# Combine before gather at the end of each expert in a two-layer mixture-of-experts step

## The chip, the cores and the metric

The kernel runs on one core of one Trainium2 chip. The metric is the device time of one execution in microseconds (us); lower is better. The median of three runs of the kernel before is 2045.48 us.

## The reference, cut to what matters

One step of a two-layer model over 288 tokens (256 of a prompt, 32 new ones of 8 sequences), all in float32. Each layer is attention and then a feed-forward part. In the second layer that part is a mixture of 8 experts, and only it is touched here: each token goes to its two best experts, and each expert adds its result, weighted by the token's gate.

```python
def moe_swiglu(h, w_router, b_router, w_in, w_out):
    logits = jnp.einsum('btd,de->bte', h, w_router, preferred_element_type=F32) + b_router.astype(F32)
    top_v, top_i = lax.top_k(logits, TOP_K)
    gates = jax.nn.softmax(top_v, axis=-1)
    dense_gate = jnp.sum(jax.nn.one_hot(top_i, N_EXPERTS, dtype=F32) * gates[..., None], axis=-2)
    out = jnp.zeros(h.shape, F32)
    for e in range(N_EXPERTS):
        out = out + dense_gate[..., e:e + 1] * swiglu(h, w_in[e], w_out[e]).astype(F32)
    return out.astype(h.dtype)
```

Sizes: D_MODEL 1024, F_EXPERT 3584, N_EXPERTS 8, TOP_K 2. The weights of one expert are 21 pieces of 2 MB.

## The kernel before, in words

The program of each engine is written out by hand, with semaphores between them. Layer 0, the attention of layer 1 and the router come first; the experts start some 930 us into the span and end near 2006 us.

**Weights.** SyncE (SP) streams the 21 pieces of each expert into 7 slots of 2 MB, 14 pieces of w_in (line 581) and then 7 of w_out (line 585). A piece is requested as soon as TensorE has used the piece that held its slot. It waits for nothing of the gather or the combine.

**One expert on TensorE** (`expert`, lines 1400 to 1423 of the kernel before):
- It waits until ScalarE and VectorE have copied the expert's gathered tokens out of PSUM (semaphores `e_gcpA`, `e_gcpV`), reads the number of its tokens into a register (`value_load`, line 1405: the instruction TENSOR_LOAD and some register work), and takes a branch to one of three bodies (lines 1420 and 1421). They stand one behind the other in the program: P for up to 128 tokens, CAP for up to 144, and a narrow one for up to 64. Every expert has its own copy of all three. So from a body to the next expert's body TensorE's instruction stream jumps over up to two bodies; only from a narrow body to a following P body does the program simply go on. At the end of a P or CAP body stands one jump more, to the end of the expert.
- The body: gate and up projections (`ffn_in`; matmuls of line 1315 in the wide bodies P and CAP, of line 1297 in the narrow one), the transposes of the choice (`turn_choice`), and the out projection (line 1365 wide, 1349 narrow).
- The end: the **gather** of the next expert's tokens, then for a wide body `out_transposes` (lines 1377 and 1379), then the **combine**.

**The gather** (lines 1257 to 1266) multiplies the stored tokens by a 0/1 choice matrix into PSUM banks 0 to 2: 24 matmuls. In float32 each one shows as two MATMUL rows and two LDWEIGHTS rows, so 48 of each. It needs only the choice (`e_pick`), which VectorE makes in the middle of the expert. `gather_copy` on ScalarE (line 1767, two copies) and on VectorE (line 2283, one) brings it to SBUF as `hsel` and counts up `e_gcpA` and `e_gcpV`.

**The combine** (lines 1382 to 1398) multiplies the expert's output by the turned choice, 8 matmuls (16 in CAP), and VectorE adds each of the 8 results to `fT` (line 2313). It starts when the output is in `otok`, scaled by the gates: ScalarE and VectorE first copy the out projection's PSUM (`oeT`: for a wide body the source of the transposes; a narrow body doesn't use it), then wait for `e_tp`, then write `otok` and count up `e_ocA` and `e_ocV`. In a wide body `e_tp` comes from the last transpose, in a narrow one from the gather's first matmul, since TensorE works in order. From the fourth combine matmul on each waits for an add, as three banks go round.

Experts 0 to 7 (e0 to e7) of this input take these bodies: P, narrow, narrow, CAP, narrow, P, narrow, narrow. The last expert also gathers once (for a ninth expert that holds no token); then the final norm follows.

Of the kernel before, what the change touches and what calls it, by code (L numbers as in the profile page):

```python
# [171 lines left out]
def build(nc, t_in, t_out):  # L172
# [12 lines left out]
    with ctx:  # L185
# [134 lines left out]
        def bank(i, n=512, at_=0, rows=P):  # L320
            return ps[0:rows, 512 * i + at_:512 * i + at_ + n]

        ident = cst[:, C_ID:C_ID + 128]
        ones = cst[:, C_ONE:C_ONE + 128]
# [39 lines left out]
        e_oeA, e_oeV, e_tp = sem("e_outT_copied_act"), sem("e_outT_copied_vec"), sem("e_out_tokens_ready")  # L364
# [316 lines left out]
        def _(pe):  # L681
            mm, tp = nc.tensor.matmul, nc.tensor.transpose
# [78 lines left out]
            for k in range(KD):  # L761
                if k >= 2:
                    pe.wait_ge(x_cp, k - 1)
                for t, (t0, n) in enumerate(TILES):
                    last = tp(bank(k % 2, n, t0), xtok[0:n, t, 128 * k:128 * k + 128], ident[0:n, 0:n])
                last.then_inc(x_tp, 1)
            pe.wait_ge(c_silu, 1)
            for k in range(KD):
                last = tp(bank(2, 9, 9 * k), cstok[:, 128 * k:128 * k + 128], ident[0:9, 0:9])
# [17 lines left out]
            for hp in range(4):  # L787
                b = t_bank()
                for q in range(4):
                    h, c = 2 * hp + q // 2, q % 2  # L790
                    last = tp(bank(b, 128, 128 * q, 64), kvb[:, c, 128 * h:128 * h + 64], ident)
# [11 lines left out]
            for j, w in enumerate((384, 288, 512, 512, 512)):  # L803
                landed("in_ab", j)
                wt = chunk("in_ab", j, 0, 8 * w).rearrange("p (k m) -> p k m", k=KD)
                for t, (t0, n) in enumerate(TILES):
                    if nz >= 4:
                        pe.wait_ge(z_cp, nz - 3)
                    for k in range(KD):
                        if nz == 0:  # L810
                            pe.wait_ge(h_done, k + 1)
                        if n < P:
                            last = sample_rows(nz % 4, hT[:, k, t0:t0 + n], wt[:, k, :], w, k, KD)
                        else:
                            last = mm(bank(nz % 4, w), hT[:, k, t0:t0 + n], wt[:, k, :], start=(k == 0), stop=(k == KD - 1))  # L815
# [22 lines left out]
            for t in range(2):  # L838
                for hh in range(2):
                    for k in range(3):  # L840
                        last = mm(bank(2 * t + hh, 384), qnT[:, k, 128 * t:128 * t + 128], wt[:, k, 384 * hh:384 * hh + 384],
                                  start=(k == 0), stop=(k == 2))
                    last.then_inc(q_done, 1)
            pe.wait_ge(q_cp, 1)
            for k in range(3):
                for g in range(4):
                    last = mm(piece(0, g, 192), qnT[:, k, NTP:NT], wt[:, k, 192 * g:192 * g + 192], start=(k == 0), stop=(k == 2))
# [315 lines left out]
            for h in range(HA):  # L1163
# [3 lines left out]
                for c in range(2):  # L1167
                    last = mm(ps[r:r + 64, 512 * (h % 4):512 * (h % 4) + NT], kvb[:, c, 128 * h + 64:128 * h + 128],
                              qlT[:, c, h, :], start=(c == 0), stop=(c == 1))
# [6 lines left out]
            for j in range(11):  # L1176
                landed("ffd_in", j)
                w = chunk("ffd_in", j, 0, 4096).rearrange("p (g k m) -> p g k m", g=2, k=KD)
                for fb in range(2):
# [3 lines left out]
                    for g in range(2):  # L1183
                        for k in range(KD):
                            if f == 0 and g == 0:
                                pe.wait_ge(h_done, 8 + k + 1)
                            last = mm(bank(2 * (f % 2) + g, NT), w[:, g, k, 128 * fb:128 * fb + 128], hT[:, k, :],  # L1187
                                      start=(k == 0), stop=(k == KD - 1))
# [7 lines left out]
            for j in range(3):  # L1196
                landed("qkv_c", j)
                wt = chunk("qkv_c", j, 0, 4096).rearrange("p (k m) -> p k m", k=KD)
                for t, (t0, n) in enumerate(TILES):
                    if nz >= 19:  # L1200
                        pe.wait_ge(z_cp, nz - 3)
                    for k in range(KD):
                        if nz == 15:
                            pe.wait_ge(h_done, 16 + k + 1)
                        if n < P:
                            last = sample_rows(nz % 4, hT[:, k, t0:t0 + n], wt[:, k, :], 512, k, KD)
                        else:
                            last = mm(bank(nz % 4), hT[:, k, t0:t0 + n], wt[:, k, :], start=(k == 0), stop=(k == KD - 1))  # L1208
# [25 lines left out]
            for t, (t0, n) in enumerate(TILES):  # L1234
                for k in range(KD):
                    if t == 0:
                        pe.wait_ge(h_done, 24 + k + 1)
                    last = mm(bank(0, 8, 8 * t, n), hT[:, k, t0:t0 + n], wrout[:, k, :], start=(k == 0), stop=(k == KD - 1))
            last.then_inc(lg_done, 1)
            for t, (t0, n) in enumerate(TILES):  # L1240
                for kk in range(2):
# [3 lines left out]
                    for k in range(4):  # L1245
                        last = tp(bank(4 + i % 2, 128, 128 * k, n), hT[:, 4 * kk + k, t0:t0 + n], ident)
                    last.then_inc(htok_tp, 1)
            pe.wait_ge(msk_done, 1)
            for t in range(3):
                for tt in range(t + 1):  # L1250
                    last = mm(bank(1, 8, 8 * t), cst[:, C_UP:C_UP + 128] if tt == t else ones, mask[:, tt, :],
                              start=(tt == 0), stop=(tt == t))
            for tt in range(3):
                last = mm(bank(1, 8, 24), ones, mask[:, tt, :], start=(tt == 0), stop=(tt == 2))
            last.then_inc(pos_done, 1)

            def gather(idx, tokens_ready=False):

                pe.wait_ge(e_pick, idx)
                for k in range(KD):  # L1260
                    for t, (t0, n) in enumerate(TILES):
                        last = mm(bank(G_BANK[k // 3], CAP, CAP * (k % 3)), htok[t][:, 128 * k:128 * k + 128],  # L1262
                                  pick[:, t, 0:CAP], start=(t == 0), stop=(t == 2))
                        if tokens_ready and k == 0 and t == 0:
                            last.then_inc(e_tp, 1)
                last.then_inc(e_gat, 1)

            def turn_choice(it, cols):
# [103 lines left out]
            def out_transposes(it, cols):  # L1372

                pe.wait_ge(e_oeA, it + 1)
                pe.wait_ge(e_oeV, it + 1)
                for k in range(KD):
                    last = tp(bank(5 + k // 4, 128, 128 * (k % 4)), oeT[:, k, 0:P], ident)
                for k in range(KD if cols > P else 0):
                    last = tp(bank(3 + k // 4, 128, 128 * (k % 4), EXTRA), oeT[:, k, P:CAP], ident)
                last.then_inc(e_tp, 1)  # L1380

            def combine(it, cols):

                pe.wait_ge(e_ocA, it + 1)
                pe.wait_ge(e_ocV, it + 1)
                for i, k in enumerate((0, 4, 1, 5, 2, 6, 3, 7)):
                    if i >= 3:
                        pe.wait_ge(e_add, NE * it + i)
                    out = bank((5, 6, 7)[i % 3], NT)
                    d = k // 4  # L1390
                    c0 = 128 * (k % 4)
                    if cols:
                        last = mm(out, otok[d][:, c0:c0 + 128], putT[0], start=True, stop=cols <= P)
                        if cols > P:
                            last = mm(out, rest_rows[:, 128 * k:128 * k + 128], rest_put, start=False, stop=True)
                    else:
                        last = mm(out, otok[0][64 * d:64 * d + 64, c0:c0 + 128], putT[0][64 * d:64 * d + 64, :], start=True, stop=True)
                    last.then_inc(e_cb, 1)

            def expert(it, e, p_):  # L1400

                pe.wait_ge(e_gcpA, it + p_ + 1)
                pe.wait_ge(e_gcpV, it + p_ + 1)
                own = cnt_i[0:1, bass.ds(e, 1)]
                tokens = pe.value_load(own, min_val=0, max_val=NT)

                def body(cols):

                    ffn_in(it, cols)
                    pe.wait_ge(e_pcp, it + 1)  # L1410
                    if cols:
                        wide_out(it, cols)
                    else:
                        narrow_out(it)
                    gather(it + p_ + 2, not cols)
                    if cols:
                        out_transposes(it, cols)
                    combine(it, cols)

                with pe.If(tokens > p_ * CAP + NARROW):  # L1420
                    with pe.If(tokens <= p_ * CAP + P):
                        body(P)
                    with pe.Else():
                        body(CAP)
                with pe.Else():
                    body(0)
# [396 lines left out]
        def _(dve):  # L1823
# [401 lines left out]
            for t, (t0, n) in enumerate(TILES):  # L2225
                last = V.max(top[0:n, t, :], logit[0:n, t, :])
# [56 lines left out]
            def gather_copy(idx):  # L2283
                dve.wait_ge(e_gat, idx)
                V.tensor_copy(hsel[:, 3:6, :], bank(G_BANK[1], 3 * CAP).rearrange("p (k n) -> p k n", k=3)).then_inc(e_gcpV, 1)

            def expert(it, e, p_, base):

                def turned_copy(j):
                    dve.wait_ge(e_t, FCH * it + (j + 1))  # L2290
                    V.tensor_copy(actT[:, j, :], bank(4, 256)).then_inc(e_tc, 1)

                for j in range(FCH):
                    if j:
                        turned_copy(j - 1)
                    if j == 4:
                        choose(e + 1, it + p_ + 1, it + 1, base)
                    for i, b in enumerate(E_BANK[j % 2]):
                        w = CAP if i else 256
                        dve.wait_ge(e_si, NFE * it + (4 * j + i + 1))  # L2300
                        out = act_b[:, j, i - 1, :] if i else act_a[:, j, :]
                        V.tensor_tensor(out, bank(b, w, 256), sil[i % 2][:, 0:w], ALU.mult).then_inc(e_act, 1)  # L2302
                turned_copy(FCH - 1)
                dve.wait_ge(e_o, FCH * it + (FCH + NMSLOT))
                V.tensor_copy(oeT[:, 3:6, :], bank(6, 3 * CAP).rearrange("p (k n) -> p k n", k=3)).then_inc(e_oeV, 1)  # L2305
                dve.wait_ge(e_pcp, it + 1)
                dve.wait_ge(e_tp, it + 1)
                V.tensor_scalar(otok[1], bank(6), gpl[:, 0:1], None, ALU.mult)
                V.tensor_scalar(otok[2][:, 512:1024], bank(4, 512, 0, EXTRA), gpl[0:EXTRA, 1:2], None, ALU.mult).then_inc(e_ocV, 1)
                gather_copy(it + p_ + 2)  # L2310
                for i, k in enumerate((0, 4, 1, 5, 2, 6, 3, 7)):
                    dve.wait_ge(e_cb, NE * it + (i + 1))
                    V.tensor_tensor(fT[:, k, :], bank((5, 6, 7)[i % 3], NT), fT[:, k, :], ALU.add).then_inc(e_add, 1)

            def pass_body(it0, p_, base):

# [63 lines left out]
```

## Time and profile before

| | us |
|---|---|
| runs: median, lowest, highest | 2045.48, 2031.88, 2050.39 |
| profiled execution: span from first to last instruction | 2039.5 |
| median of the runs less that span | 6.0 |
| TensorE matmul busy | 1827.6 (90%) |
| VectorE, ScalarE busy | 418.7 (21%), 334.0 (16%) |
| chain that ended last: TensorE, DMA | 73%, 12% |
| mean granted TensorE clock, share of full speed | 0.953 |

The time of a run holds the span and what lies around it. The profile gives the span of the profiled execution alone, so the distance to the median of the runs stands for the rest.

How to read it: a busy share is an average over stages with different limits. In a chain of waits each piece begins where what released it ended; "issue" in it is time in which TensorE waited for nothing that shows as an engine's work. PE is the matmul side of TensorE, PEld its weight loads, PEldq its instruction sequencer, which handles waits, register loads and branches. DVE is VectorE, ACT is ScalarE. A timeline merges equal instructions: start, length, count, and in brackets how long the engine had stood idle and what ended that.

### The profile page before, as it was taken

How to read it: one execution, taken by the hardware profiler on the slowest of the kernel's cores; microseconds unless marked ns; L12 is line 12 of the kernel's file. 1: busy time of each engine (PE TensorE's matmuls, PEld its weight loads, DVE VectorE, ACT ScalarE, POOL GpSimd, SP SyncE). 2: the span in 40 equal slices, each digit the busy share in tenths (PEclk: the TensorE clock that was granted, in tenths of full speed). 3: DMA queues.
4: the chain of work that ended last, by engine and by line, in shares of the span. 5: the costliest groups of instructions: out<-in, count | busy, mean ns of one | idle time of the engine just before them, and what ended most of it. 6: DMA issues, size and time to landing. Idle time of an engine off the chain costs nothing.

```text
span 2039.5 us, 30167 instructions
## 1 busy us (share of the span) xinstructions
PE 1827.6 (90%) x12873; PEld 1354.7 (66%) x12874; DVE 418.7 (21%) x1260; ACT 334.0 (16%) x1000; POOL 53.2 (3%) x99
## 2 busy tenths in 40 slices
PE   6799899899999997988998979789989899988874
PEld 3455566667777745768997636389976499954532
DVE  1114333340000034642101211101012111021213
ACT  2122334230000123621000101000001000011102
POOL 1002120000000000000000000000000000000000
PEclk9998999799999997888999999989999999989997
DMA  9943866454334562052785999986749998869991
GB/s 352 366 135 109 274 215 226 150 190 141 124 105 128 165 211 80 31 218 83 278 314 194 385 397 388 402 326 248 289 167 355 399 361 311 307 239 402 386 401 40
DMA packets 252023, 504.30 MB, mean 247 GB/s; under 512 B 6953, under 2 KB 65497, under 8 KB 251746
## 3 DMA queue, kind: packets, MB, share of 16 engines
q1 hardware_dynamic: 248066, 495.49, 67.4%
q0 software_dynamic: 3808, 6.61, 1.1%
q8 instruction: 119, 1.95, 0.4%
q14 instruction: 30, 0.25, 0.0%
HBM read 499.05 MB, written 3.02 MB: 246 GB/s over the span
## 4 chain that ended last, share of the span: by engine, by line
PE 73%; DMA 12%; SPq 6%; issue 3%; DVE 3%; ACT 1%; POOL 0%; DVEq 0%
PE ps L1315 15%; PE ps L1187 8%; PE ps L1297 8%; PE ps L1365 8%; PE ps L755 7%; DMA big<-in_w_moe_out 6%; SPq L585 4%; PE ps L815 3%; DMA big<-in_w_ada 3%; PE ps L1262 3%; PE ps L1208 2%; DMA big<-in_w_moe_in 2%; PE ps L704 2%; PE ps L917 1%; PE ps L1349 1%
## 5 line engine op out<-in xcount | busy, mean ns | idle before, releaser
L1315 PE MATMUL ps<-big 128*128 128x128 f32 (+1 forms) x2688 | 315.7, 281 | 9.1 <-issue 9.1
L1315 PEld LDWEIGHTS ps<-big 128*128 128x128 f32 x2688 | 314.6, 193 | 10.2 <-issue 10.2
L1297 PE MATMUL ps<-big 128*64 128x256 f32 x2240 | 262.3, 392 | 45.0 <-issue 35.1
L1297 PEld LDWEIGHTS ps<-big 128*64 128x64 f32 x2240 | 163.1, 141 | 133.6 <-issue 51.3
L1187 PE MATMUL ps<-work,big 128*128 128x288 f32 x704 | 171.2, 406 | 1.0 <-ACT work L1462 1.0
L1462 ACT ACTIVATE gqkv<-ps 128x144 f32<-128x144 f32 (+1 forms) x231 | 66.5, 315 | 619.2 <-PE ps L1315 300.9
L2302 DVE TENSOR_TENSOR z<-ps,gqkv 128x256 f32<-128x256 f32 x224 | 69.0, 334 | 460.7 <-ACT gqkv L1462 460.7
L1349 PE MATMUL ps<-big,z 128*64 128x512 f32 x560 | 127.7, 598 | 38.2 <-DMA big<-in_w_moe_out 35.2
L1187 PEld LDWEIGHTS ps<-work,big 128*128 128x128 f32 x704 | 133.6, 190 | 38.3 <-issue 1.5
L1365 PE MATMUL ps<-z,big 128*128 128x128 f32 (+1 forms) x1344 | 155.6, 279 | 2.3 <-issue 2.3
L1365 PEld LDWEIGHTS ps<-z,big 128*128 128x128 f32 x1344 | 155.1, 191 | 2.8 <-issue 2.8
L1462 ACT ACTIVATE z<-ps 128x288 f32<-128x288 f32 (+5 forms) x107 | 43.9, 426 | 576.0 <-PE ps L1349 159.9
L1349 PEld LDWEIGHTS ps<-big,z 128*64 128x64 f32 x560 | 37.8, 136 | 122.1 <-issue 63.9
L704 PE MATMUL ps<-big,csT 128*32 128x256 f32 x576 | 67.5, 388 | 21.6 <-DMA big<-in_w_ada 20.1
L755 PE MATMUL ps<-z,big 128*128 128x288 f32 x352 | 85.6, 406 | 1.0 <-DVE z L2181 1.0
L1462 ACT ACTIVATE big<-ps 128x384 f32<-128x384 f32 (+11 forms) x137 | 56.0, 432 | 167.0 <-PE ps L704 63.7
L755 PEld LDWEIGHTS ps<-z,big 128*128 128x128 f32 x352 | 66.8, 190 | 19.8 <-DVE z L2181 1.4
L1462 ACT ACTIVATE work<-ps 128x288 f32<-128x288 f32 (+4 forms) x104 | 38.3, 394 | 193.3 <-PE ps L755 137.3
L704 PEld LDWEIGHTS ps<-big,csT 128*32 128x32 f32 x576 | 35.0, 112 | 49.3 <-DMA big<-in_w_ada 14.1
L755 PE MATMUL ps<-o_or_q,big 128*128 128x288 f32 x256 | 65.2, 418 | 0.6 <-ACT o_or_q L1462 0.6
L2305 DVE COPY z<-ps 128x432 f32<-128x432 f32 x8 | 4.9, 608 | 290.7 <-PE ps L1365 148.1
L815 PE MATMUL ps<-big,work 128*128 128x512 f32 (+2 forms) x160 | 60.6, 537 | 3.3 <-ACT work L1462 3.3
(319 smaller groups left out, 1646.4 us busy)
## 6 DMA issues: line engine op xcount, KB each, us to landing
big<-in_w_moe_in SPq DMA_DIRECT2D x112, 2048.0 KB, 15.6
big<-in_w_moe_out SPq DMA_DIRECT2D x56, 2048.0 KB, 19.6
big<-in_w_ada SPq DMA_DIRECT2D x24, 2048.0 KB, 13.6
big<-in_w_ffd_in SPq DMA_DIRECT2D x22, 1024.0 KB, 7.7
big<-in_w_ffd_out SPq DMA_DIRECT2D x8, 1408.0 KB, 7.0
big<-in_cache_b_k SPq DMA_DIRECT2D x4, 2048.0 KB, 8.1
big<-in_cache_mla_ckv SPq DMA_DIRECT2D x64, 128.0 KB, 4.2
big<-in_cache_b_v SPq DMA_DIRECT2D x4, 2048.0 KB, 11.9
```

The lines of the kernel that those rows point to most:

```text
L585: sp.dma_start(wslot(q).rearrange("p (f m) -> p f m", f=4), src).then_inc(e_in[q], 16)
L704: last = mm(ps[CB * g:CB * g + CB, 512 * b:512 * b + WA], csT[:, k, :], w[:, k, WA * g:WA * g + WA], start=(k == 0), stop=(k == KD - 1))
L755: last = mm(bank(4 + k % 2, NT), w[:, f, 128 * m:128 * m + 128], rhs[:, f, :], start=(f == 0), stop=(f == nk - 1))
L815: last = mm(bank(nz % 4, w), hT[:, k, t0:t0 + n], wt[:, k, :], start=(k == 0), stop=(k == KD - 1))
L1187: last = mm(bank(2 * (f % 2) + g, NT), w[:, g, k, 128 * fb:128 * fb + 128], hT[:, k, :], start=(k == 0), stop=(k == KD - 1))
L1262: last = mm(bank(G_BANK[k // 3], CAP, CAP * (k % 3)), htok[t][:, 128 * k:128 * k + 128], pick[:, t, 0:CAP], start=(t == 0), stop=(t == 2))
L1297: last = mm(ps[64 * a:64 * a + 64, 512 * b + 256 * g:512 * b + 256 * g + 256], hsel[:, k, 0:NARROW], w[:, k, 256 * a:256 * a + 256], start ...
L1315: last = mm(bank(b, cols, 256 * g), w[g][:, k, 128 * i:128 * i + 128], hsel[:, k, 0:cols], start=(k == 0), stop=(k == KD - 1))
L1349: last = mm(ps[64 * d:64 * d + 64, 512 * 5:512 * 6], actT[:, q, 128 * m + 64 * half:128 * m + 64 * half + 64], w[:, i, 512 * d:512 * d + 5 ...
L1365: last = mm(bank(5 + k // 3, cols, CAP * (k % 3)), w[:, i, 128 * k:128 * k + 128], act, start=(q == 0 and i == 0 and k % 3 == 0), stop=(q ...
L1462: return nc.scalar.activation(out, in_, f, **kw)
L2302: V.tensor_tensor(out, bank(b, w, 256), sil[i % 2][:, 0:w], ALU.mult).then_inc(e_act, 1)
```

## The change

At the end of every body TensorE now works out_transposes (wide bodies), then the combine, then the gather, so that the gather's matmuls stand directly ahead of the branch to the next expert. As the gather's first matmul came behind the narrow out projection and gave `e_tp`, a narrow body now has one small matmul of 4 columns in its place. VectorE does its 8 adds before its copy of the gather; ScalarE's order is unchanged.

```diff
-            def gather(idx, tokens_ready=False):
+            def gather(idx):
 
                 pe.wait_ge(e_pick, idx)
                 for k in range(KD):
                     for t, (t0, n) in enumerate(TILES):
                         last = mm(bank(G_BANK[k // 3], CAP, CAP * (k % 3)), htok[t][:, 128 * k:128 * k + 128],
                                   pick[:, t, 0:CAP], start=(t == 0), stop=(t == 2))
-                        if tokens_ready and k == 0 and t == 0:
-                            last.then_inc(e_tp, 1)
                 last.then_inc(e_gat, 1)
...
                         wide_out(it, cols)
                     else:
                         narrow_out(it)
-                    gather(it + p_ + 2, not cols)
                     if cols:
                         out_transposes(it, cols)
+                    else:
+                        mm(bank(4, 4), ident, ones[:, 0:4], start=True, stop=True).then_inc(e_tp, 1)
                     combine(it, cols)
+                    gather(it + p_ + 2)
...
                 V.tensor_scalar(otok[2][:, 512:1024], bank(4, 512, 0, EXTRA), gpl[0:EXTRA, 1:2], None, ALU.mult).then_inc(e_ocV, 1)
-                gather_copy(it + p_ + 2)
                 for i, k in enumerate((0, 4, 1, 5, 2, 6, 3, 7)):
                     dve.wait_ge(e_cb, NE * it + (i + 1))
                     V.tensor_tensor(fT[:, k, :], bank((5, 6, 7)[i % 3], NT), fT[:, k, :], ALU.add).then_inc(e_add, 1)
+                gather_copy(it + p_ + 2)
```

TensorE at the end of a narrow body, here of e4, and at the start of e5, before the change. 64x512 are the last matmuls of the out projection, 128x144 those of the gather, 128x288 those of the combine; in brackets the semaphores that an instruction waits for.

```order
L1349 MATMUL ps<-big,z 64x512 x7
L1262 MATMUL ps<-o_or_q,work 128x144 [waits pick_ready]
L1262 MATMUL ps<-o_or_q,work 128x144
...
L1397 MATMUL ps<-big,work 128x288 [waits e_out_copied_vec,e_out_copied_act]
L1397 MATMUL ps<-big,work 128x288 x2
L1397 MATMUL ps<-big,work 128x288 [waits combine_added] x5
L1425 UNCONDITIONAL_BRANCH
L1405 TENSOR_LOAD work [waits gather_copied_vec,gather_copied_act]
```

The same place with the change.

```order
L1347 MATMUL ps<-big,z 64x512 x7
L1416 MATMUL ps<-cst 128x4
L1395 MATMUL ps<-big,work 128x288 [waits e_out_copied_vec,e_out_copied_act]
L1395 MATMUL ps<-big,work 128x288 x2
L1395 MATMUL ps<-big,work 128x288 [waits combine_added] x5
L1262 MATMUL ps<-o_or_q,work 128x144 [waits pick_ready]
L1262 MATMUL ps<-o_or_q,work 128x144
...
L1262 MATMUL ps<-o_or_q 128x144
L1425 UNCONDITIONAL_BRANCH
L1403 TENSOR_LOAD work [waits gather_copied_vec,gather_copied_act]
```

The gather (24 matmuls) has moved from ahead of the combine to behind it; the read of the count still waits for the gather's copies, and these now follow the last thing that TensorE does in the body.

VectorE at the end of the first expert, before and with the change as one piece of the difference: L2308 and L2309 write `otok`, L2285 copies the gather, the eight 128x288 are the adds.

```order
 L2308 TENSOR_SCALAR work<-ps,work 128x512
 L2309 TENSOR_SCALAR work<-ps,work 16x512
+L2312 TENSOR_TENSOR work<-ps,work 128x288 x8
 L2285 COPY big<-ps 128x432
-L2313 TENSOR_TENSOR work<-ps,work 128x288 x8
 L2302 TENSOR_TENSOR z<-ps,gqkv 128x256
```

The copy of the gather has moved behind the adds, as the gather has on TensorE.

## Rows read from the trace of the kernel before

**Rows 1.** Page, head: the span of the profiled execution.

```profile
span 2039.5 us, 30167 instructions
```

**Rows 2.** Timeline, TensorE, end of e0 (P) and start of e1 (narrow).

```profile
1101.35 1.04 PE L1377 MATMUL ps<-cst,z 128*128 128x128 f32 x8
1104.04 4.12 PE L1393 MATMUL ps<-big,work 128*128 128x288 f32 x16 [1.65 <-DVE work L2309]
1115.73 1.55 PE L1297 MATMUL ps<-big 128*64 128x256 f32 x6 [7.58 <-issue]
```

**Rows 3.** Chain that ended last, end of e1 (narrow): start us, us, what.

```profile
1202.49 6.08 PE ps L1262 x48
...
1209.80 2.41 PE ps L1397 x10
1212.21 6.37 issue
1218.58 4.60 PE ps L1297 x27
```

**Rows 4.** The same chain behind the combines of e2, e3, e4, e5.

```profile
1325.23 6.61 issue
...
1519.69 6.33 issue
...
1623.54 0.39 issue
...
1789.03 7.35 issue
```

**Rows 5.** By source line, TensorE's sequencer, e0, e1, e3: ns min/median/max, first and last start.

```profile
L1421 PEldq COMPARE_BRANCH  x1: 3639/3639/3639, 1107.2 to 1107.2; - x1
...
L1420 PEldq COMPARE_BRANCH  x1: 3941/3941/3941, 1111.7 to 1111.7; - x1
...
L1405 PEldq TENSOR_LOAD <-work x1: 311/311/311, 1211.6 to 1211.6; - x1
...
L1420 PEldq COMPARE_BRANCH  x1: 6287/6287/6287, 1212.2 to 1212.2; - x1
...
L1423 PEldq COMPARE_BRANCH  x1: 3641/3641/3641, 1517.3 to 1517.3; - x1
```

**Rows 6.** Windows: DMA and granted clock at e0/e1, over e2, behind the router's gather.

```profile
core 0: us, PE busy (x) PEld busy (x) DVE busy (x) ACT busy (x) POOL busy (x), PEclk, DMA share, GB/s
1104.20:1120.00 15.80, 8.22 (x42) 5.31 (x43) 3.87 (x9) 0.23 (x1) 0.00 (x0) 0.78 0.02 4
...
1198.80:1311.90 113.10, 91.06 (x649) 51.84 (x649) 17.85 (x52) 10.94 (x38) 0.00 (x0) 0.97 1.04 394
...
941.50:944.90 3.40, 3.40 (x16) 3.40 (x17) 0.00 (x0) 0.00 (x0) 0.00 (x0) 0.50 0.00 0
...
1204.10:1208.00 3.90, 3.90 (x34) 3.90 (x33) 0.35 (x1) 0.39 (x1) 0.00 (x0) 1.00 1.05 387
```

**Rows 7.** Timeline, ScalarE at the end of e1: the `oeT` copies, then `otok`.

```profile
1202.54 0.83 ACT L1462 ACTIVATE z<-ps 128x432 f32<-128x432 f32 x2 [30.60 <-PE ps L1349]
...
1203.26 1.23 ACT L1462 ACTIVATE work<-ps,work 128x512 f32<-128x512 f32 x2
```

**Rows 8.** Timeline behind the router's gather, ahead of e0: its copies, e0's first matmuls.

```profile
939.32 0.83 ACT L1462 ACTIVATE big<-ps 128x432 f32<-128x432 f32 x2 [11.25 <-PE ps L1262]
...
941.42 0.92 PE L1315 MATMUL ps<-big 128*128 128x128 f32 x3 [2.14 <-issue]
```

**Rows 9.** A wait on TensorE's sequencer in e0, and the chain there.

```profile
L1279 PEldq EVENT_SEMAPHORE  x1: 2865/2865/2865, 1042.4 to 1042.4; - x1
...
1044.60 0.77 issue
```

**Rows 10.** Timeline, e2: the first matmuls that wait for weights.

```profile
1265.15 3.67 PE L1297 MATMUL ps<-big 128*64 128x256 f32 x32 [1.38 <-DMA big<-in_w_moe_in]
```

**Rows 11.** Timeline behind the last combine: ScalarE's squares, VectorE's first step of the final norm.

```profile
2006.95 2.77 ACT L1462 ACTIVATE work<-work 128x288 f32<-128x288 f32 x8 [3.30 <-DVE work L2313]
2008.13 0.35 DVE L1879 TENSOR_SCALAR work<-work,coef 128x256 f32<-128x256 f32 x1 [1.22 <-ACT work L1462]
```

## The prediction

> **What bounds the kernel now.** I read the head of the page for the span [rows 1], then the chain of waits through the experts, then the ends of single experts in the timeline, and last the rows of TensorE's own sequencer. In the chain the reader is to see that behind nearly every combine TensorE stands idle for 6.3 to 7.6 us under the name "issue" [rows 2 to 4]; behind e4 alone it is 0.39 us [rows 4], and e4, a narrow body, is the one that a P body follows, so that nothing is jumped over. The sequencer's rows say what "issue" is: a taken branch. The one at the end of e0 took 3.64 us and the one into e1's narrow body 3.94 us, both while the weight stream stood still (a DMA share of 0.02); the one from e1 into e2 took 6.29 us, with the stream at full load (1.04) [rows 5, 6]. The change removes none of these jumps; what counts is when each can begin.
>
> Two facts decide that. First, the sequencer runs ahead of the matmuls where nothing holds it: it stood at a wait at 1042.4 while the matmuls ahead of that wait ended at 1044.60, 2.2 us later [rows 9], and at the end of e3 it took its branch at 1517.3 while the combine ended at 1519.69, 2.4 us later [rows 4, 5]. I use 2.3 us. In e0's combine the waits for the adds hold it longer: its branch came at 1107.2, 0.95 us ahead of the combine's end at 1108.15 (7.58 ahead of 1115.73) [rows 2, 5]. Second, it can't read the next count before the gather's copies are done. Before the change these are long done when the combine ends.
>
> The weights matter too. From the end of e1 to that of e2 the DMA share is 1.04 throughout [rows 6], and e2 waits for its weights from 1265.15 on [rows 10]: a later start of e2 is caught up in these waits. e6 and e7 stand to each other in the same way (two narrow bodies in a row). All other ends have a wide body on one side or the final norm behind, and there a delay goes into the time.
>
> **The change part by part.** Nothing is removed but the order; 5 matmuls of 4 columns are added, which I cost at nothing, since ScalarE's `oeT` copies cover them (0.83 us [rows 7]).
>
> *What the gather hid.* Before, its 6 us lay over the copies of the out projection. Now they stand open.
> - Narrow: the out projection of e1 ends at 1202.49; `otok` is written from 1203.26 for 1.23 us, so until 1204.49, and 0.15 us later the combine can start: 2.1 us in which TensorE waits [rows 3, 7].
> - Wide: one pair of `oeT` copies, 0.83 us (the same copies as in rows 7), and some 0.3 us of latencies and lost overlap: 1.1 us. The wait behind the transposes, 1.65 us, stood open before [rows 2].
>
> So the combine and the gather together end 2.1 us (narrow) or 1.1 us (wide) later than before.
>
> *What now stands ahead of the branch.* With the gather last, the read of the count comes 0.9 us behind the gather's end: two copies of ScalarE, 0.83 us, with latencies [rows 8].
> - Narrow, with a jump: before, the read began at 1211.6, 0.6 us ahead of the end at 1212.21 [rows 3, 5]. Now it begins 0.9 us behind an end that is itself 2.1 us later: 0.6 + 0.9 + 2.1 = 3.6 us. The jump is as long as before, as the stream is at full load there before and after.
> - Narrow with no jump (e4): the same 3.6, and the 2.14 us of idle that the router's gather shows between gather and body [rows 8] hold 0.2 us more than the read took in e4: 3.8.
> - P: the jump at the end now stands behind matmuls that wait for nothing but the choice, so the sequencer comes to it 2.3 us ahead of the gather's end instead of 0.95 ahead of the combine's. Its start moves by 1.1 - 2.3 + 0.95 = -0.25 us. It takes 3.64, so it ends 1.3 us behind the gather, when the copies (0.9) are done: they cost nothing here. Everything behind it is as before: -0.3 each.
> - CAP: there the sequencer was 2.4 us ahead already: 1.1 - 2.3 + 2.4 = +1.2.
> - Behind e7: ScalarE now copies the gather before its squares. The combine ended near 2006.1, so the gather ends near 2008.2 and the copies at 2009.1, against squares from 2006.95 [rows 11]. VectorE's start moves by about as much: +2.1.
>
> The nearest row for the run-ahead is the one of e3, at the same kind of place; the bounds are that none of it comes (the jump starts with the gather's end, and a P end costs +2.0 instead of -0.3) and that all of it is hidden (the read starts 0.9 behind the gather, -0.7).
>
> The Trainium skill, "Advanced Engine Details and Errata", section "Engine Queue Depths", gives TensorE a queue of 64 instructions. The gather is 96 rows in 5.9 us, so 64 of them would let the sequencer be about 3.9 us ahead, an estimate from that page; the rows show 2.2 to 2.4. By the page the three wide ends would each be 0.6 us shorter and the sum 1.8 us smaller; I stay with the rows.
>
> *The clock.* After the long gaps it is at 0.5 before and after alike. But the new waits are new idle time in a stretch that ran at 1.00 [rows 6]. After the 2.14 us of idle behind the router's gather the clock stood at 0.50 for 3.4 us [rows 6, 8], which costs 1.7 us of work; after the 1.65 us in e0 it did not fall before the next long gap, and over e2, with its many waits for weights (the first 1.38 us [rows 10]), its mean is 0.97. My new idles are 2.1 us at e2, e4 and e7, 2.1 us ahead of e5's body, and at e0 and e5 1.0 and 1.65 us close together. So 0 to 6 times 1.7 us, and as they lie nearest to the row of 2.14 but not surely alike, I take three: 5.1 us.
>
> *Sum.* e0 and e5 -0.6, e2 +3.6, e3 +1.2, e4 +3.8, e7 +2.1, clock +5.1: about +15 us. e1 and e6 (+3.6 each) cost nothing as long as the weights cover them. On the span of 2039.5 that makes 2054.5; the median of the runs lies 6.0 above this span, so 2060.5. Without the clock it would be +10, with all six falls +20.
>
> **The rivals.**
> 1. *The sequencer doesn't get ahead of the gather* (or the jump into the next body gets longer). For it: the gather is short pieces with a weight load each, and no row shows the sequencer passing just these. Against it: rows 5 and 9. The three wide ends then cost 2.3 us more each, and up to 3.6 if the fetch also waits on the copies: +7 to +11, so about 2070.
> 2. *The weights don't cover e1 and e6.* For it: e2 has slack only until 1265. Against it: it comes to the weights' pace 46 us behind its start at 1218.58 and goes at that pace for 46 us more, up to 1311.9. +7.2: about 2068.
> 3. *Not slower: the branch is taken during the gather.* Were the count read and the jump begun while the gather still runs, its 6 us would cover the fetch at every end. A narrow end with a jump would then take 2.1 + 3.6 + 6 + 0.9, some 12.7 us instead of 16.1 (1202.49 to 1218.58 [rows 3]): -3.4 at e2. At a wide end 1.1 + 0.9 stand in place of the idle behind the combine [rows 4]: -5.6 and -5.4 at e0 and e5, -4.3 at e3. With e4 (2.1 + 0.9 for 0.39, +2.6) and e7 (+2.1) still dearer the sum is -14 us: 2031.5. It decides where the read of the count doesn't wait for the copies. For it: the first jump of a wide end does come early. Against it: the order shows the read waiting for both copies, and behind the router's gather the body began only 2.14 us later with no jump at all [rows 8].
>
> **How the numbers follow.** My forecast, +15 with +8 to +21 as its own range, gets 0.70; the first rival 0.12, the second 0.08, the third 0.06; 0.04 is left for what I don't see. The range reaches from 2046 (little loss of clock, quick fetches) to 2076 (the first rival with most falls of the clock); the runs of before alone are 18 us apart. Over 1%, some 20 us, is about what a measurement of this kernel can tell from no change. The forecast lies under it, so its upper end (0.08) and the two slow rivals make slower 0.28; the third rival's -14 is within 1%, and faster gets 0.03; the same 0.69.
>
> **What would show it.** In the profile of the changed kernel: the combine of a narrow body starts 2.1 us behind the out projection; the count is read 0.9 us behind the gather's end, never before; the branch at the end of e0 begins some 2.3 us ahead of that end and takes 3.6; idle between gather and next body is about 8 us behind e1 and e2 (0.9, 0.7 for the read, 6.3), 6 us behind e0, 2.1 us behind e4; e2 and e7 end no later against their predecessors than before. I am wrong if the branch into a body starts before the gather's copies are done, if the fetches change their length, or if e2's end moves with its start.

## The result, and the profile after

The changed kernel takes 2057.55 us (median of 4 runs, 2053.88 to 2066.97) against 2040.8 us before (4 runs, 2031.88 to 2050.39): the medians are 16.75 us apart, a quotient of 1.0082, and the ratio on record is 1.0101 with a 95% interval of 1.0055 to 1.0148. Measured again beside other kernels on one chip (6 runs against 17, below) the ratio is 1.0102, 1.0078 to 1.0125, with medians of 2061.51 and 2036.93, 24.6 us apart. The ratio on record is not the quotient of the medians, and the record does not say how it is formed; by either the kernel is about 1% slower. The span of the profiled execution went from 2039.5 [rows 1] to 2054.3 us, by 14.8. The time of that same execution is 2055.88, only 1.6 us above its span; the 6.0 us that the forecast put between span and time were for the most part the spread of the runs.

The end of e1 in the chain of waits of the changed kernel, to be held against [rows 3] (start us, us, what):

```profile
1196.21 3.68 PE ps L1347 x16
...
1200.34 0.40 ACT z L1462
1200.74 1.13 ACT work L1462 x2
1201.87 0.10 issue
1201.97 0.78 PE ps L1395 x4
...
1203.24 2.41 PE ps L1395 x10
1205.65 6.09 PE ps L1262 x48
...
1212.19 0.41 ACT big L1462
1212.61 7.04 issue
1219.65 2.40 PE ps L1295 x9
```

ScalarE's copies now stand in the chain, first those of the out projection (2.1 us from 1199.89 to the combine at 1201.97), then those of the gather; before, the gather lay over the ones and the combine over the others. From the end of the out projection to the next body's first matmul it is 19.8 us, where it was 16.1. The sequencer's rows behind it, and the jump at the end of e0, answer to [rows 5] (ns min/median/max, first and last start):

```profile
L1421 PEldq COMPARE_BRANCH  x1: 3472/3472/3472, 1104.6 to 1104.6; - x1
...
L1403 PEldq TENSOR_LOAD <-work x1: 308/308/308, 1212.6 to 1212.6; - x1
...
L1420 PEldq COMPARE_BRANCH  x1: 6205/6205/6205, 1213.4 to 1213.4; - x1
```

The count is read at 1212.6, 0.9 us behind the gather's end (1205.65 + 6.09 = 1211.74), and the jump behind it is as long as it was (6.2). At the end of e0 the jump starts at 1104.6, while the gather runs on to 1106.98; it is done 1.1 us behind it. The end of e0 in the timeline, against [rows 2]:

```profile
1096.97 4.12 PE L1391 MATMUL ps<-big,work 128*128 128x288 f32 x16 [1.65 <-DVE work L2309]
...
1113.18 1.12 PE L1295 MATMUL ps<-big 128*64 128x256 f32 x4 [6.21 <-issue]
```

The idle ahead of e1 is 6.21 instead of 7.58 us; most of the difference stands ahead of the combine now, where the copies of the out projection are open: behind the out projection combine and gather together take 13.67 us (1093.31 to 1106.98) instead of 12.52 (1095.63 to 1108.15), 1.15 more.

This table has, for every expert, the time from the end of its out projection to the next body's first matmul (for e7: to the end of the span), worked out from the timelines of the two profiles in the same way (the changes from hundredths).

| end | body, next body | before | after | change | forecast |
|---|---|---|---|---|---|
| e0 | P, narrow | 20.1 | 19.9 | -0.2 | -0.3 |
| e1 | narrow, narrow | 16.1 | 19.8 | +3.7 | +3.6, covered |
| e2 | narrow, CAP | 16.3 | 20.0 | +3.6 | +3.6 |
| e3 | CAP, narrow | 23.6 | 24.2 | +0.6 | +1.2 |
| e4 | narrow, P | 10.1 | 16.3 | +6.2 | +3.8 and clock |
| e5 | P, narrow | 19.9 | 22.8 | +2.9 | -0.3 and clock |
| e6 | narrow, narrow | 16.1 | 19.8 | +3.7 | +3.6, covered |
| e7 | narrow, final norm | 42.8 | 45.0 | +2.2 | +2.1 |

The cover held: from the end of e1's out projection to that of e2's it is 113.0 us in both profiles, and the weight stream runs at a share of 1.04 over that stretch in both [rows 6]. In what follows a fall is a stretch in which the granted clock is at 0.50, the lower of its two levels (1.2 and 2.4 GHz). The clock's part is seen in windows of the changed kernel (busy us and count of PE, PEld, DVE, ACT, POOL, then granted clock, DMA share, GB/s), to be held against [rows 6]:

```profile
1618.30:1625.00 6.70, 6.70 (x23) 5.06 (x22) 3.31 (x8) 0.00 (x0) 0.00 (x0) 0.50 1.05 387
...
1631.90:1635.20 3.30, 3.30 (x17) 3.30 (x17) 0.00 (x0) 0.00 (x0) 0.00 (x0) 0.50 1.05 387
1788.90:1795.60 6.70, 6.05 (x13) 4.36 (x14) 2.79 (x6) 0.34 (x1) 0.00 (x0) 0.50 0.64 244
```

The clock is at 0.50 in e4's combine and the start of its gather, at the start of e5's body and in e5's combine. In the chain these two ends read:

```profile
1617.47 4.84 PE ps L1395 x16
1622.31 7.45 PE ps L1262 x48
...
1789.55 7.16 PE ps L1391 x16
1796.71 5.89 PE ps L1262 x48
```

In e1 the same pieces took 3.68 and 6.09 us, and in e0 the combine 4.12: 2.5 us lost at e4 and 3.0 at e5. e5's body took 154.2 us instead of 152.6, 1.6 more. So of the 14.8 us, 7.1 are these three falls, and -0.2 + 3.6 + 0.6 + 3.7 (e4 without its fall) - 0.1 (e5 without its fall) + 2.2 = 9.8 are the order; the rest, -2, lies where the change isn't: e0's body had a fall of 1.6 in the profile before [rows 6] and none in the one after, and the experts began 0.7 us earlier.

### The profile page after: what moved, and what is told of

Its sections match the earlier page's. It is cut to its first block, busy times and chain, and to the rows that moved or that the text cites. A ratio compares the mean times of both kernels' runs of the same rounds, so it can differ in the third digit from the quotient of the medians.

```text
span 2054.3 us, 30187 instructions
## 1 busy us (share of the span) xinstructions
PE 1833.2 (89%) x12883; PEld 1362.7 (66%) x12884; DVE 419.5 (20%) x1260; ACT 334.4 (16%) x1000; POOL 53.3 (3%) x99
## 3 DMA queue, kind: packets, MB, share of 16 engines
q0 software_dynamic: 3808, 6.61, 1.1%
## 4 chain that ended last, share of the span: by engine, by line
PE 71%; DMA 12%; SPq 8%; issue 4%; DVE 3%; ACT 2%; POOL 0%; DVEq 0%; ACTq 0%
PE ps L1313 15%; PE ps L1187 8%; PE ps L1363 8%; PE ps L1295 7%; PE ps L755 7%; DMA big<-in_w_moe_out 6%; SPq L585 5%; DMA big<-in_w_ada 3%; PE ps L815 3%; PE ps L1262 3%; PE ps L1208 2%; DMA big<-in_w_moe_in 2%; PE ps L704 1%; PE ps L1347 1%; PE ps L1395 1%
## 5 line engine op out<-in xcount | busy, mean ns | idle before, releaser
L1313 PEld LDWEIGHTS ps<-big 128*128 128x128 f32 x2688 | 314.6, 193 | 12.7 <-issue 12.7
L755 PEld LDWEIGHTS ps<-z,big 128*128 128x128 f32 x352 | 66.8, 190 | 19.8 <-DVE z L2181 1.4
L704 PEld LDWEIGHTS ps<-big,csT 128*32 128x32 f32 x576 | 34.7, 112 | 50.6 <-DMA big<-in_w_ada 14.8
```

Source lines behind the costliest of these rows:

```text
L704: last = mm(ps[CB * g:CB * g + CB, 512 * b:512 * b + WA], csT[:, k, :], w[:, k, WA * g:WA * g + WA], start=(k == 0), stop=(k == KD - 1))
L755: last = mm(bank(4 + k % 2, NT), w[:, f, 128 * m:128 * m + 128], rhs[:, f, :], start=(f == 0), stop=(f == nk - 1))
L1313: last = mm(bank(b, cols, 256 * g), w[g][:, k, 128 * i:128 * i + 128], hsel[:, k, 0:cols], start=(k == 0), stop=(k == KD - 1))
```

## The experiments

**x1: the read of the count no longer waits for the gather's copies.**

```diff
-                pe.wait_ge(e_gcpA, it + p_ + 1)
-                pe.wait_ge(e_gcpV, it + p_ + 1)
                 own = cnt_i[0:1, bass.ds(e, 1)]
...
                 def body(cols):
 
+                    pe.wait_ge(e_gcpA, it + p_ + 1)
+                    pe.wait_ge(e_gcpV, it + p_ + 1)
                     ffn_in(it, cols)
```

> The changed kernel, with the wait for the gather's copies moved from ahead of the read of the count to the start of the next body. My theory: in the changed kernel the read is held by these copies, 0.9 us behind the gather's end. Without that wait it begins some 2.3 us ahead of the gather's end, as far as the sequencer gets ahead of the matmuls. A narrow end with a jump (e1, e2, e6: 19.7 to 20.0 us from the end of the out projection to the next body's first matmul) gets 3.2 us shorter, about 16.6; e4's end, with no jump, 1 to 1.3 us shorter without its clock loss; P and CAP ends stay within 0.3 us, since there the jump at the end of the body is what the read waits for. The time falls by some 4 to 5 us against the changed kernel, before the clock. Rival (the branch hides the whole fetch under the gather as soon as nothing holds the read): narrow ends 12.7 us, P ends 14.5 us. Rival (the read waits for the matmuls whatever the semaphores say): nothing changes.

One run: 2049.58 us, the kernel before beside it 2040.23. The end of e6 in the chain, and its read:

```profile
1895.88 6.09 PE ps L1262 x48
...
1902.84 3.87 issue
1906.70 3.65 PE ps L1295 x15
```

```profile
L1401 PEldq TENSOR_LOAD <-work x1: 306/306/306, 1899.6 to 1899.6; - x1
```

The read comes at 1899.6, 2.4 us ahead of the gather's end at 1901.97, and the end takes 16.6 us instead of 19.8, as my theory had it. The sequencer gets no further ahead than that, so the rival's 12.7 us is out, and so is the one that reads only behind the matmuls. The other ends are harder to tell: e0, e1, e2, e4 and e5 each had a fall here, and e1 and e2 took 19.4 us with theirs. The idle behind the gather shows the read's part all the same: at e0 and e5 it is 6.42 and 5.91 us, where the changed kernel has 6.21 and 6.10, so that the free read gives nothing there; ahead of e5's body it is 0.92 instead of 1.93. e3's end took 24.8, 0.6 more than in the changed kernel's first profile and outside what I expected; x8, which has no such edit, has 24.8 there too.

**x2: the same in the kernel before.** The edit of x1, made to the kernel before.

> The kernel before, with the same wait moved behind the branch. My theory: there the read is held not by the copies but by the combine's last wait for an add, so nothing moves: 20.1, 16.1, 16.3, 23.6, 10.1, 19.9, 16.1 us at the ends of e0 to e6, each within 0.3. Rival (the copies hold it in the kernel before too): the narrow ends get 1 to 2 us shorter.

One run: 2031.85 us beside 2040.23, within what single runs differ by. The ends of e0 to e6 took 19.9, 16.1, 16.3, 23.7, 10.1, 20.1 and 16.1 us: nothing moved. With the combine last it is not the copies of the gather that hold the sequencer. What is left are the combine's waits for the adds; that they do is argued from the order of the program, and no run took them out.

**x3: VectorE's half of the change alone.** `gather_copy` of VectorE behind its adds, TensorE as before.

```diff
-                gather_copy(it + p_ + 2)
                 for i, k in enumerate((0, 4, 1, 5, 2, 6, 3, 7)):
                     dve.wait_ge(e_cb, NE * it + (i + 1))
                     V.tensor_tensor(fT[:, k, :], bank((5, 6, 7)[i % 3], NT), fT[:, k, :], ALU.add).then_inc(e_add, 1)
+                gather_copy(it + p_ + 2)
```

> The kernel before, with VectorE's copy of the gather moved behind its 8 adds and TensorE's order as it was: the VectorE half of the change alone. My theory: the copy now ends some 0.45 + 0.6 us behind the combine, so the read of the count begins 1.1 us behind the combine's end and not 0.6 ahead of it: +1.7 us at the narrow ends (e1, e2, e4, e6: 17.8, 18.0, 11.8, 17.8 us); nothing at P and CAP ends, where the jump at the end of the body takes longer. On the time +3 to +4 us (e2 and e4; e1 and e6 are covered by the weights). Rival (the read isn't held by that semaphore): nothing moves.

One run: 2049.32 us beside 2040.23; the experts began 6 us later in this profile than in that of before, which the edit can't reach. The end of e1 in the chain:

```profile
1216.07 2.06 PE ps L1397 x8
1218.13 0.02 issue
1218.15 0.82 DVE work L2312 x2
1218.97 0.52 DVE big L2285
1219.50 7.13 issue
```

VectorE's copy now stands in the chain, behind the adds. The narrow ends took 17.9, 18.1, 11.9 and 17.8 us, the P and CAP ends 20.7, 23.6 and 19.7: +1.8 where the read is next, little where a jump stands ahead of it (e0's 0.6 us lies in jumps that took 3.79 and 4.39 instead of 3.64 and 3.94). From e0's first matmul to the end of the span this profile takes 1100.0 us, that of before 1098.1, of which 1.6 are its fall at e0: 3.5 more, where I expected 3 to 4. So the price of a held read is shown by itself.

**x4 and x9: the new idle times filled.** The changed kernel with matmuls whose results are not used, so that TensorE isn't idle there.

```diff
+            def fill(b, n):
+                for _ in range(n):
+                    mm(bank(b, 128), ident, ones, start=True, stop=True)
...
                     if cols:
+                        fill(0, 3)
                         out_transposes(it, cols)
+                        fill(0, 6)
                     else:
                         mm(bank(4, 4), ident, ones[:, 0:4], start=True, stop=True).then_inc(e_tp, 1)
+                        fill(0, 8)
                     combine(it, cols)
                     gather(it + p_ + 2)
+                    if not cols:
+                        fill(3, 8)
```

> The changed kernel, with small matmuls of no use put into its new idle times: 8 of 128 columns behind a narrow out projection and 8 behind a narrow body's gather, 3 and 6 around a wide body's transposes. They fill about 1.9, 1.9, 0.7 and 1.5 us and none is on the path. My theory: the clock falls at e4's combine, ahead of e5's body and at e5's combine come from the new idles; filled, the clock stays at 1.00 there, e4's end takes 13.6 to 13.9 us instead of 16.3, e5's body 152.6 instead of 154.2, e5's end 19.8 instead of 22.8: the span falls by about 7 us against the changed kernel, to some 2047. Rival (the falls have nothing to do with these idles): falls remain at such places, and the span stays near 2054.

One run: 2048.75 us beside 2040.23, span 2047.1. e4's end took 13.9 us, e5's body 152.6, e5's end 19.5. The clock stood at 1.00 over e4's end, at e5's start and over e5's end:

```profile
1615.70:1630.00 14.30, 14.04 (x102) 12.32 (x103) 5.71 (x12) 2.78 (x6) 0.00 (x0) 1.00 1.05 386
1630.00:1633.40 3.40, 3.40 (x33) 3.40 (x32) 0.00 (x0) 0.00 (x0) 0.00 (x0) 1.00 1.05 387
1782.20:1796.00 13.80, 13.04 (x90) 11.64 (x88) 5.79 (x12) 2.21 (x5) 0.00 (x0) 1.00 0.43 155
1329.80:1338.80 9.00, 6.68 (x26) 6.33 (x27) 0.00 (x0) 0.00 (x0) 0.00 (x0) 0.50 1.05 387
```

The last row is one I had not expected. Behind e2 the 8 matmuls keep TensorE at work 2 us longer into the gap, and the clock, which in the changed kernel is at 0.50 for the first 5.5 us of e3's body, is so for the first 9.1 here. But in the row the matmuls are busy for 6.68 of its 9 us only. The timeline shows why:

```profile
1329.79 3.46 PE L1317 MATMUL ps<-big 128*128 128x144 f32 x13 [6.32 <-issue]
1335.57 14.63 PE L1317 MATMUL ps<-big 128*128 128x144 f32 x104 [2.32 <-issue]
```

Behind the body's first 13 matmuls TensorE stands idle for 2.32 us under the name "issue"; in the changed kernel the first 142 run without a gap. The body took 173.7 us instead of 170.5. Of these 3.2 us the stop is 2.3; the low clock, under which TensorE works for 6.8 us instead of 5.5, costs half of the difference, 0.7. What makes the stop was not tried.

That the span fell to the 2047.1 that I expected is luck in part: the experts began 4.6 us earlier than in the changed kernel's profile (936.13 against 940.72). From e0's first matmul to the end of the span the two take 1111.0 and 1113.6 us. The three places gave back 7.4 us, as expected; e3's body took 3.2 of it, and a fall at the start of e0's body, which this profile has and the other not, 1.6.

Both kernels were then timed on one chip.

> The changed kernel once more, on the chip of the next run, for its time beside that of the filled kernel. My theory: the open copies and the later read cost 9.6 us in every execution, and the clock some 0 to 10 us more, as the new idle times meet it: a ratio of 1.007 to 1.009 over the kernel before. In its profile the segments stay (19.8 us at narrow ends with a jump, 19.9 at P ends without a fall), and the places of the falls may be others than in the first profile. Rival (the falls are tied to the places): the same three places again.

> The filled kernel of x4, now timed. My theory: without the clock's part it stands some 9 to 10 us over the kernel before, a ratio of 1.0045 to 1.005, and 3 to 7 us under the changed kernel beside it; no fall in its profile behind an out projection, at a combine or between e4's gather and e5's body. Rival (the useless matmuls cost as much as the clock they keep): the same time as the changed kernel.

| kernel | median (lowest to highest), runs | ratio to before | 95% interval |
|---|---|---|---|
| changed (x8) | 2061.51 (2055.65 to 2062.55), 6 | 1.0102 | 1.0078 to 1.0125 |
| changed, filled (x9) | 2049.27 (2040.28 to 2057.76), 12 | 1.0061 | 1.0039 to 1.0083 |
| before | 2036.93 (2027.32 to 2046.22), 17 | | |

Of the 1.0% the filling takes 0.4 back, some 8 us (12 between the medians). In the profiles, from e0's first matmul to the end, x8 takes 1117.5 us, x9 1109.1 and the kernel before 1098.1. I had expected a ratio of 1.0045 to 1.005 and 3 to 7 us less than the changed kernel, so both came out larger. What is left, 0.6% or 12 us, is the 9.8 of the order and the 3 us at e3: x9's profile has 173.5 us there, with a stop of 2.31 us behind the first 13 matmuls. In x8's profile, without filling, the falls stood at the same three places as in the first profile and at two more:

```profile
1621.00:1627.70 6.70, 6.70 (x23) 5.02 (x22) 3.37 (x8) 0.00 (x0) 0.00 (x0) 0.50 1.05 385
1634.70:1638.00 3.30, 3.30 (x17) 3.30 (x17) 0.00 (x0) 0.00 (x0) 0.00 (x0) 0.50 1.05 387
1791.70:1798.40 6.70, 6.12 (x13) 4.43 (x14) 2.72 (x6) 0.27 (x1) 0.00 (x0) 0.50 0.63 241
1904.30:1911.00 6.70, 6.66 (x23) 5.38 (x24) 2.82 (x7) 0.00 (x0) 0.00 (x0) 0.50 1.05 388
2016.90:2023.70 6.80, 6.77 (x24) 5.30 (x24) 3.00 (x8) 0.00 (x0) 0.00 (x0) 0.50 0.00 0
```

The two more are e6's end (covered by the weights) and e7's (not covered). x1, with the same idles ahead of its combines, had falls at e0, e1 and e2 too. So my ratio of 1.007 to 1.009 was a little low, and whether the three places come back in every execution stays open: two profiles of the changed kernel had them, and there are no more.

**x5: the gather in two parts.** 15 of its 24 matmuls stand ahead of the combine as before, 9 behind it. In a narrow body the first of them gives `e_tp` again.

```diff
...
+                    gather(it + p_ + 2, 0, 5, not cols)
                     if cols:
                         out_transposes(it, cols)
-                    else:
-                        mm(bank(4, 4), ident, ones[:, 0:4], start=True, stop=True).then_inc(e_tp, 1)
                     combine(it, cols)
-                    gather(it + p_ + 2)
+                    gather(it + p_ + 2, 5, KD)
```

> The gather in two parts: its first 15 matmuls (k 0 to 4) where the kernel before has the gather, the last 9 (2.2 us) behind the combine; the rest as in the changed kernel, with the read of the count behind the gather's copies. My theory: the first part hides the copies of the out projection, so combine and gather together end where they ended before (12.5 us behind the out projection at a P end, 9.7 at a narrow one); the read still comes 0.9 us behind the gather's end. So from the out projection's end to the next body: narrow 17.6 (16.1 before, 19.8 with the change), e4 11.9 (10.1, and 13.9 with the change without its clock loss), P 18.7 (20.1 and 19.8), CAP 23.6 (23.6 and 24.2). No clock falls at e4 or at the combines. Span about 1 us over the kernel before. Rival (what is dear is the order, combine ahead of any of the gather, not the open copies): the narrow ends stay near 19.8.

One run: 2039.78 us, beside 17 runs of the kernel before with a median of 2034.91. Ends of e0 to e6: 19.2, 17.9, 18.0, 23.6, 11.9, 18.4, 17.8 us. The 15 matmuls hide the copies, the combine starts at once, and the rival's 19.8 is out: it was the open copies. e0's end is 0.5 above the 18.7 that I expected. One miss: I expected no fall of the clock at e4, and one came at the start of e5's body, behind the 1.95 us of idle between this gather's end and that body (1621.80 to 1623.75 in the chain); e5's body took 154.2 us.

```profile
1619.38 2.42 PE ps L1263 x18
...
1622.66 1.09 issue
1623.75 2.42 PE ps L1317 x16
```

```profile
1625.30:1628.60 3.30, 3.30 (x18) 3.30 (x17) 0.00 (x0) 0.00 (x0) 0.00 (x0) 0.50 1.05 387
```

**x6: x5 with the read set free as in x1.**

> x5 with the wait for the gather's copies moved behind the branch. My theory: nothing then holds the sequencer in the last 2.2 us of a body: the read begins 2.3 us ahead of the gather's end. Narrow ends 14.5 us (16.1 before), P 18.6, CAP 23.6, e4 10.7 (its first matmul now waits for the copies themselves). Against the kernel before e0 and e5 -1.5 each, e2 -1.6, e3 0, e4 +0.6, e7 +0.4: about -3.5 us. Rival (a jump taken while matmuls run takes longer by as much): the narrow ends stay near 16.

One run: 2032.01 us, beside the same 17. Ends: 18.8, 14.6, 14.8, 23.8, 10.8, 18.5, 14.5 us. The end of e2 in the chain, and its read:

```profile
1316.08 2.42 PE ps L1263 x18
...
1319.36 3.97 issue
1323.33 2.74 PE ps L1317 x10
```

```profile
L1405 PEldq TENSOR_LOAD <-work x1: 304/304/304, 1316.0 to 1316.0; - x1
```

The read comes 2.5 us ahead of the gather's end at 1318.49, and the jump runs while matmuls do: 4.8 us of idle where the kernel before has 6.61 [rows 4]. Against the kernel before the ends of e0, e2 to e5 sum to -1.3 - 1.5 + 0.2 + 0.7 - 1.4 = -3.3 us. That is too little for its single time to tell.

**x7: x6 with all counts read ahead of e0.**

```diff
-                own = cnt_i[0:1, bass.ds(e, 1)]
-                tokens = pe.value_load(own, min_val=0, max_val=NT)
+                tokens = counts[e] if isinstance(e, int) else pe.value_load(cnt_i[0:1, bass.ds(e, 1)], min_val=0, max_val=NT)
...
+            counts = [pe.value_load(cnt_i[0:1, e:e + 1], min_val=0, max_val=NT) for e in range(3)]
             gather(1)
+            counts += [pe.value_load(cnt_i[0:1, e:e + 1], min_val=0, max_val=NT) for e in range(3, NE)]
```

> x6 with the counts of all 8 experts read once, ahead of the first expert, so that no read stands ahead of a branch. My theory: every end with a jump gets the read's 0.65 to 0.75 us shorter than in x6: narrow 13.8, P 17.9, CAP 22.9, e4 10.7. Against the kernel before about -6.5 us, a ratio near 0.997; the timing can hardly tell that from no change, the profile can. Rival (the jump's fetch begins only when the matmuls ahead of it have ended): no gain over x5.

2034.51 us (12 runs) against 2034.91 (17): a ratio of 0.9992, 0.9972 to 1.0013, no change that can be told, and no version of this study that beats the kernel before measurably. The narrow ends are 13.9 and 14.1 us as expected, but P and CAP ends gained nothing (19.1, 23.8, 18.7). Their second jump, now directly behind the first, takes longer:

```profile
L1422 PEldq COMPARE_BRANCH  x1: 4937/4937/4937, 1110.4 to 1110.4; - x1
...
L1423 PEldq COMPARE_BRANCH  x1: 3747/3747/3747, 1106.6 to 1106.6; - x1
```

4.94 us, against 4.31 in x6 and 3.94 in [rows 5], both with a read in between. What holds the second jump was not tried. And the early reads are not free: TensorE is idle for 4.89 us ahead of the router's gather, where it was 3.90 before and in x6, and from that gather's start to e0's first matmul it is 10.06 us instead of x6's 9.15. So x7 pays some 1.9 us ahead of e0, which I had not counted.

## Why the prediction was right, point by point

- **The forecast.** +15 us, 2060.5; measured +16.75 between the medians, 2057.55, ratio 1.0101, and +14.8 between the spans. The sign and most of the size, 9.8 of the 14.8 us, came from the order as it was said (10.1). That the whole fits so well is luck in part: the clock cost 2.0 us more than its term, and some 2 us were gained where the change is not.
- **The open copies and the held read** (+3.6 at a narrow end): +3.6 and +3.7 in the profile. x5 removes the one, x1 the other, x3 adds the read's wait to the kernel before; each moved the narrow ends by about what its part was said to cost (1.9, 3.2 and 1.8 us).
- **The sequencer 2.3 us ahead.** At the ends of e0, e3 and e5 the jump starts 2.35 us ahead of the gather's end, at e0 at 1104.6 against 1106.98. The rows were right to follow. The 3.9 us that were worked out, as an estimate, from the queue of 64 that the Trainium skill gives ("Advanced Engine Details and Errata", section "Engine Queue Depths") did not show in any run. The sum that the prediction hung on it is wrong besides: by its own terms the read would then wait for the copies, 0.9 us behind the gather instead of 1.34, so a wide end would be 0.45 us shorter, not 0.6, and the sum 1.3 us smaller. The first rival, no lead at all, is out: P ends moved by -0.2.
- **The cover of the weights.** The end of e2's out projection did not move against that of e1's, nor e7's against e6's (113.0 and 112.8 us, 113.0 and 112.9 before). The second rival is out.
- **The branch taken during the gather,** the third rival: out by the read at 1212.6; and x1 shows that even a free read would have given 3 us at a narrow end and nothing behind the gather of a P end; the lead of 2.4 us was as far as the sequencer got.
- **CAP** (+1.2): +0.6 in the first profile, where its two jumps took 3.28 and 3.86 instead of 3.64 and 4.16; +1.2 in x8's, with jumps of 3.57 and 4.25. The order's term fits; the length of a jump varies by some tenths, and two profiles can't tell more.
- **The clock** (+5.1, three falls of 1.7): this is the term that was mis-sized. Three falls it was, but those at e4 and in e5's combine lasted 6.8 us and cost 2.5 and 3.0; with the 1.6 at e5's start 7.1 us in the first profile, and 9.3 in x8's, with the 2.2 of e7's; there e6's body took 1.7 more besides, most of it as it began with 7.4 us at 0.50 instead of 4.1. That the idles cause them is shown by x4 and x9, where they are filled and the falls gone. But the number three was a choice between none and six, not worked out, and such an idle makes a fall possible, not certain: in x3 2.20 us ahead of e5's body were followed by none (the clock is at 1.00 from 1539.84 to 1802.67), and ahead of e0's body seven profiles have 2.12 to 2.16 us, of which three (before, x4 and x5) have a fall behind it and four (the changed kernel's two, x3 and x9) have none. What decides between them stays open.

## What to carry to other kernels

Work that stands in front of a jump covers it only if the instruction stream can get past that work: what the branch or the register read ahead of it waits for must be done earlier. Here the gather's place covered copies on one side and its own copies on the other, and moving it opened both; ask of a piece that is to be moved what it hides where it is. And a new idle time of two microseconds on TensorE may be paid twice, once itself and once in the clock behind it; in one execution it is and in the next it may not be.

## What the runs showed that I had not expected

- A jump directly behind another took longer than one with 0.65 us of register work between: at the ends of e0, e3 and e5 the second took 4.94, 4.77 and 5.03 us in x7, and 4.31, 4.58 and 4.01 in x6.
- Work put into a gap can cost more behind the gap: e3's body took 173.7 and 173.5 us in x4 and x9 against 170.5, some 0.7 us of it by a fall of the clock that lasted longer into the body, 2.3 by a stop behind its first 13 matmuls that the changed kernel does not have.
- The lead of the sequencer is the same at all these places: 2.35 to 2.45 us where matmuls of the gather are last, 2.2 and 2.4 us in [rows 5, 9].
